# Last column group of the up projections in the merged form, first half of the down projections in a turning bank

## The reference, cut to what matters

```python
D_MODEL, SEQ, D_FF = 1024, 256, 2816
def conv_ffn(h, w_up, conv_w, conv_b, w_down):      # FFN 0 and 1
    gu = h @ w_up                                    # 1024 -> 2 * 2816
    g, u = gu[..., :D_FF], gu[..., D_FF:]
    g = depthwise_causal_conv(g, conv_w) + conv_b
    return (jax.nn.silu(g) * u) @ w_down             # 2816 -> 1024
def swiglu(x, w13, w2):                              # FFN 2 to 5
    gate, up = jnp.split(x @ w13, 2, axis=-1)
    return (jax.nn.silu(gate) * up) @ w2
```

## Time and profile before

| | us |
|---|---|
| median of 3 runs | 2125.82 |
| lowest and highest | 2122.11 and 2129.02 |
| the profiled execution | 2125.66 |
| its span in the profile | 2123.9 |

### The profile page before, as it was taken

How to read it: one execution, slowest core, us unless ns; L and a number is a source line. 1 busy time by engine, 2 the same in 40 slices (tenths; PEclk the granted TensorE clock), 3 DMA queues, 4 the chain that set the end, 5 groups by cost and what they waited for, 6 DMA issues and landing times.

```text
span 2123.9 us, 34246 instructions
## 1 busy us (share of the span) xinstructions
PE 2067.6 (97%) x14836; PEld 1801.3 (85%) x14836; DVE 1433.9 (68%) x1652; ACT 1055.2 (50%) x1256; POOL 155.4 (7%) x119
## 2 busy tenths in 40 slices
PE   8899999999999999999999999999999999999998
PEld 7888888988888888998778888888889977788887
DVE  7966766567765664876766776476558576678654
ACT  4545554655643553455544455345435564444542
POOL 1000000000001000330000010020005200002000
PEclk9799999999999999999999999999999999999999
DMA  7254655435555665563402466566546533135653
GB/s 186 40 169 153 198 189 172 156 119 179 179 188 189 197 199 178 186 206 126 139 23 100 156 205 195 188 189 198 180 161 217 197 119 119 43 119 167 210 189 129
DMA packets 259789, 342.45 MB, mean 161 GB/s; under 512 B 23383, under 2 KB 169469, under 8 KB 259639
## 3 DMA queue, kind: packets, MB, share of 16 engines
q1 hardware_dynamic: 254272, 329.95, 47.7%
q0 software_dynamic: 2768, 9.08, 1.5%
q10 hardware_dynamic: 2599, 1.23, 0.5%
HBM read 338.14 MB, written 2.10 MB: 160 GB/s over the span
## 4 chain that ended last, share of the span: by engine, by line
PE 77%; DVE 14%; ACT 4%; DMA 3%; issue 1%; POOL 0%; ACTq 0%; SPq 0%; DVEq 0%
PE acc L1969 10%; PE acc L1971 10%; PE acc L1970 10%; PE trp L2139 9%; PE acc L2139 7%; DVE w_lo L1244 5%; PE trp L2140 4%; PE acc L2140 4%; PE acc L1985 3%; PE trp L1969 2%; PE trp L1971 2%; PE trp L1970 2%; ACT w_hi L750 2%; PE acc L2034 1%; PE acc L2186 1%
## 5 line engine op out<-in xcount | busy, mean ns | idle before, releaser
L1244 DVE TENSOR_TENSOR w_lo<-raw,w_hi 128x2048 fp32r<-128x2048 f32 (+1 forms) x312 | 721.4, 2315 | 400.3 <-ACT w_hi L750 398.5
L750 ACT ACTIVATE w_hi<-raw 128x2048 fp32r<-128x2048 f32 (+1 forms) x312 | 586.2, 1880 | 526.3 <-PE acc L1971 182.0
L2139 PE MATMUL trp<-xT,w_hi 128*128 128x512 f32 x960 | 339.5, 398 | 0.8 <-DVE w_lo L1244 0.8
L2139 PE MATMUL acc<-xT,w_hi 128*128 128x512 f32 x768 | 271.3, 397 | 0.0
L2140 PE MATMUL trp<-xT,w_lo 128*128 128x256 f32 x960 | 268.9, 280 | 0.0
L2139 PEld LDWEIGHTS trp<-xT,w_hi 128*128 128x128 f32 x960 | 180.3, 188 | 45.6 <-issue 1.7
L2140 PE MATMUL acc<-xT,w_lo 128*128 128x256 f32 x768 | 215.1, 280 | 0.0
L1969 PE MATMUL acc<-w_hi,hT_hi 128*128 128x512 f32 x528 | 205.5, 389 | 0.0
L1970 PE MATMUL acc<-w_lo,hT_hi 128*128 128x512 f32 x528 | 205.5, 389 | 0.0
L1971 PE MATMUL acc<-w_hi,hT_lo 128*128 128x512 f32 x528 | 205.4, 389 | 0.0
L1969 PE MATMUL acc<-xT,w_hi 128*128 128x256 f32 x704 | 199.9, 284 | 3.5 <-DVE w_lo L1244 3.4
(11 more groups left out here) (436 smaller groups left out, 3430.8 us busy)
## 6 DMA issues: line engine op xcount, KB each, us to landing
raw<-in_ffn_w SPq DMA_DIRECT2D x184, 512.0 KB
raw<-in_w_in SPq DMA_DIRECT2D x60, 1024.0 KB
raw<-in_ffn_w_up SPq DMA_DIRECT2D x88, 512.0 KB
raw<-in_ffn_w SPq DMA_DIRECT2D x40, 1024.0 KB
raw<-in_ffn_w_down SPq DMA_DIRECT2D x20, 1024.0 KB
raw<-in_ssm_w_glu SPq DMA_DIRECT2D x16, 512.0 KB
raw<-in_kv_w SPq DMA_DIRECT2D x8, 1024.0 KB
raw<-in_w_branch_a SPq DMA_DIRECT2D x8, 1024.0 KB
```

The lines of the kernel that those rows point to most:

```text
L750: A(w_hi[:, p % SPL, 0:kt, :], raw[:, p % RAW, 0:kt, :], ACT.Copy).then_inc(hi_ready, 1)
L1244: V_.tensor_tensor(w_lo[:, p % SPL, 0:kt, :], raw[:, p % RAW, 0:kt, :], w_hi[:, p % SPL, 0:kt, :].bitcast(F32), ALU.subtract).then_inc(lo_ ...
L2139: mm(tile, w_hi[:, p % SPL, k, c], xT[:, k0 + k], start=i == k == 0, stop=False, skip_group_check=True)
```

## The change

Group 10 of all six up projections takes the merged form: it fills both `acc`, is folded like the groups before it, and uses one more number of `acc`. The first half of each down projection (j = 0 of `tokens`) no longer has a number of `acc`. It accumulates in `turn_banks[0]`, waits before its first matmul until group 9 is folded, and is released by `turn_freed`, for which TensorE also waits at the end of the FFN. The number of uses of `acc` per FFN stays the same, and so does the accumulator that the second half takes.

```diff
--- before.py
+++ after.py
@@ -50,7 +50,7 @@
 RAW, SPL = 2, 3
 TRP = 4
 
-MERGED = range(1, 10)
+MERGED = range(1, 11)
 
 TWO_PI = 2 * math.pi
 MAGIC = 1.5 * 2 ** 23
@@ -390,6 +390,15 @@
                     filled[n_use] = (panel_used, ps[-1] + 1)
                     n_use += 1
 
+        def down_uses(name):
+
+            nonlocal n_use
+            turns.append((name, 0))
+            pairs_at[name, 0] = None
+            pairs_at[name, 1] = n_use
+            filled[n_use] = (panel_used, gemms[name][1][-1] + 1)
+            n_use += 1
+
         def place(name, j):
 
             return pairs_at[name, j] if (name, j) in pairs_at else use[name] + j
@@ -404,7 +413,7 @@
         use["y"] = n_use
         n_use += 2
         gemm_uses("glu")
-        up_uses("up0"), gemm_uses("down0")
+        up_uses("up0"), down_uses("down0")
         spots = {}
 
         def turn_spot(name, k):
@@ -420,9 +429,9 @@
             turn_spot(f"rem{i}", 0), turn_spot(f"rem{i + 1}", 1), uses(f"rem{i + 2}", 1), uses(f"rem{i + 3}", 1)
         uses("oT", 2)
         gemm_uses("o")
-        up_uses("up1"), gemm_uses("down1")
+        up_uses("up1"), down_uses("down1")
         for i in range(DEPTH):
-            up_uses(f"up{2 + 2 * i}"), gemm_uses(f"down{2 + 2 * i}")
+            up_uses(f"up{2 + 2 * i}"), down_uses(f"down{2 + 2 * i}")
             uses(f"win{i}", SIDE, f"win{i}")
             uses(f"bdT{i}", 1), uses(f"bd{i}", 1), uses(f"G{i}", 1)
             for n in range(8 + 2):
@@ -441,7 +450,7 @@
                     uses(f"Z{i}_{lv}_{t}", 1)
             uses(f"dl{i}", 7)
             gemm_uses(f"brB{i}"), gemm_uses(f"wo{i}")
-            up_uses(f"up{3 + 2 * i}"), gemm_uses(f"down{3 + 2 * i}")
+            up_uses(f"up{3 + 2 * i}"), down_uses(f"down{3 + 2 * i}")
 
         def side_panel(i, n):
 
@@ -531,7 +540,11 @@
             return f * len(MERGED) + j - MERGED.start + 1
 
         def A2(u):
-            return acc[u % 2][:, :].rearrange("p (t n) -> p t n", t=2)
+            return (turn_banks[0] if u is None else acc[u % 2])[:, :].rearrange("p (t n) -> p t n", t=2)
+
+        def turn_no(name, j):
+
+            return turns.index((name, j)) + 1
 
         def A8(u):
             return acc[u % 2][:, :].rearrange("p (h m) -> p h m", h=8)
@@ -1335,6 +1348,14 @@
                     return V_.scalar_tensor_tensor(xs, xs, scale, A2(u)[:, ts], ALU.mult, ALU.add)
 
                 def evacuate(j, u):
+                    if u is None:
+                        dve.wait_ge(panel_used, gemms[name][j][-1] + 1)
+                        if nat is not None:
+                            dve.wait_ge(sem("xnat_ready"), naturals[nat] + 1)
+                        add(u, j, slice(0, TT)).then_inc(sem("turn_freed"), 1)
+                        dve.wait_ge(sem("turn_freed"), turn_no(name, j))
+                        statistics(j)
+                        return
                     if j < len(gemms[name]) - 1:
                         wait_filled(dve, u)
                         if nat is not None:
@@ -2019,7 +2040,10 @@
             def tokens(name, j, u, src, ready=None, arriving=None):
 
                 out = A2(u)
-                claim(u)
+                if u is None:
+                    pe.wait_ge(sem("turn_freed"), turn_no(name, j) - 1)
+                else:
+                    claim(u)
                 for i, p in enumerate(gemms[name][j]):
                     pe.wait_ge(lo_ready, p + 1)
                     _, _, k0, kt, _ = panels[p]
@@ -2148,8 +2172,9 @@
                     else:
                         features(f"up{f}", j, place(f"up{f}", j), xs, arriving=Arriving(xname))
                 for j in range(2):
-                    tokens(f"down{f}", j, use[f"down{f}"] + j, hT,
+                    tokens(f"down{f}", j, place(f"down{f}", j), hT,
                            lambda k0, kt: pe.wait_ge(sem("hlo_ready"), f * 11 + (k0 + kt) // 2))
+                pe.wait_ge(sem("turn_freed"), turn_no(f"down{f}", 0))
 
 
             pe.wait_ge(sem("ident_in"), 16)
```

## The result

The changed kernel takes 2128.67 us (median of 22 runs, 2125.23 to 2131.57), the kernel before 2125.9 beside it: ratio 1.0013, interval 1.0007 to 1.0019. It is 2.8 us slower, where 0.14 us less was forecast. Measured again beside other kernels it came to 1.0017 (1.0009 to 1.0026).

What follows compares the result with a forecast made beforehand. TensorE was taken to bound the kernel, with VectorE setting FFN 0's end. FFN 1 to 4 at -0.84, FFN 5 at -0.40 and FFN 0 at +1.1 gave -0.14 us against 2125.66: 2125.5 us, range 2121.5 to 2129.5.

Steps and rivals of the forecast that it cites:

- D2's stall: FFN 0's down projection, first half: TensorE waits 0.3 to 0.5 us for the late split of its third weight panel.
- the tail of FFN 0: End of FFN 0, which hangs on VectorE: its first addition comes 0.6 to 1.9 us later than 348.55.
- the tail of FFN 1: End of FFN 1: delayed loads regain 1.6 us before the end; loss 0, with 0.5 us as upper bound.
- Part 1: Groups 10 of six FFN: 96 matmuls become 64 each, gaining 1.49 us in all if TensorE sets the end.
- Part 3: Down projection's first half in the turning bank: costs 0, bound 0.05 us per FFN above and below.
- Part 2, FFN 0: Group 10's fold in FFN 0 delays a split by 1.93 us; loss 1.1 us, ends -0.1 and +3.1.
- the ring: Weight loads and splits releasing each other, 9.3 us a lap; in FFN 0 its delay was to reach the end.
- D4's load: Load of the down projection's fifth panel, 6.28 us in FFN 0: at 5.0 the delay is 0.65, at 6.28 1.93.
- Part 2, FFN 1: Group 10's fold in FFN 1, margin about 1 us at the third panel: cost 0, at most 0.5 us.
- nothing moves: Rival for the whole kernel: neither fold nor form shows, half-clock stretches come and go; 2124 to 2127.5 us, within 0.05.
- The weight loads: Rival: weight loads bind group 10, each group gives back 1.72 us, six times 10.3: 2115.3 us; chance 0.03.
- The clock rival: Rival: the new TensorE stall in FFN 0 halves the granted clock, costing 6.8 us: 2132.3 us; chance 0.05.

Runs made afterwards that it cites:

- the bank alone: Kernel before with all groups 10 plain and only the first half of every down projection accumulating in the turning bank: ratio 1.0003 (0.9995 to 1.0012).

## Why the prediction was wrong

Against the sum of the prediction, in means of the profiles: the groups 10 gave -1.69 (forecast -1.49), D2's stall and the tail of FFN 0 +1.62 (+1.35, which is the loss of 1.1 without the gain of 0.25), the tail of FFN 1 +0.87 (0), layer 0's mixer +4.82 (no term), and everything else -2.52 (no term), of which -1.89 is the rate of the merged pairs and -0.54 layer 1's mixer. Together +3.1 for -0.14. So two steps failed: FFN 1's tail was taken at nothing, and the stages behind the FFN were taken as unchanged. The measured 2128.67 us lies inside the stated range of 2121.5 to 2129.5 us, but only because that range was as wide as the spread of single runs; it bears out none of the mechanisms.

**Part 1** held: 0.21 in FFN 1 and 2, 0.21 or 0.42 in FFN 3 to 5 by the rate of the pairs, and 1.3 to 1.7 in all for 1.49.

**Part 3** held: the bank alone is 1.0003. Its use (without it the first half of each down projection lasts 1.8 to 6.4 us longer, the 6.4 with 6.8 us at half clock in it) was not in my text, since the trace of before can't show it.

**Part 2, FFN 0** held in mechanism; the size is partly luck: D2's split at 300.46 (300.42 forecast), the first half of the down projection 0.45 us longer (stall of 0.3 to 0.5 forecast), the delay carried by the ring. In the first profile little of the delay arrives: D4's load took 4.91 us, near the end of the range at which I had put the delay at 0.1, and the first addition is 0.31 us late. The tail brings another 0.0 to 2.6, by profile, and 1.7 of the 2.6 is a stretch at half clock. With the gain of group 10 the mean is -0.3 + 0.5 + 1.1 = +1.3, for +1.1; without that stretch it is +0.7.

**Part 2, FFN 1** failed: I took 0, at most 0.5, "a ring delayed by 1.6 us regains that before the end". D2's split starts 1.94 us later in relation to group 9's end, the last one 0.77 later in relation to group 10's, and the next stage 0.6 to 1.3 later. ScalarE's idle time of 4.38 us was not the slack of the ring. It ended with a slot of TensorE, but the load had landed only 0.96 us earlier, at 654.81: so 0.96 us was the slack, for a delay of 1.9 us. Idle time shows how long an engine has nothing to do, not how early its other input lay ready. I had named the signature, the tail of FFN 0 in FFN 1, as what would prove me wrong.

**What was not in the sum at all** is the largest term: the place of the instruction fetches, +4.8 us in layer 0 with the half clock that came with it. I priced an instruction removed by what it costs in the stream where it stands. The profile of before had the hint: in both delta rules TensorE waits 1.7 us for "issue" among the small matmuls, once each, four matmuls apart in their order. With 64 instructions fewer per group such waits had to move, and with them up to 4 us for each layer. A rival of that size on either side was missing; "nothing moves" held only the half-clock stretches, and took them as chance: up to 1.7 us each way.

**The weight loads and the clock.** The weight loads don't bind: group 10 kept 11.31 us. The clock rival didn't come as told: the stall at D2 left the clock at 1.00 in the stretch around it. Stretches of 3.4 us at half clock did come in other places, behind the hole in layer 0, once in the input projection and once behind FFN 0 (at 358.2 us).

I wrote that 0.3% is about what a measurement can tell. 22 runs of each told 0.13% with an interval of 0.06 on either side; for the sizes that this change deals in, that was the bound to think in.

## What to carry to other kernels

An edit that changed TensorE's number of instructions shifted the borders of its fetch blocks through all that followed, and cost time 200 us away from the edit. Where the stream is dense with tiny instructions, look in the profile for idle time that ends in "issue", and test the edit at two or three shifts before it is called slower or faster. A null edit, a whole block of increments, is the control.

Idle time in front of an instruction is slack only as long as its second input is early: look at what else it waits for, and when that arrived.

Where a loss has a new wait in it, look at the granted clock behind the wait too: here the half clock added nearly as much as the hole itself.

## What the runs showed of the hardware

The place of an instruction fetch among small matmuls. 64 instructions without work on TensorE cost 6.6 us (1.0031), 256 cost none that can be told (1.0001). The waits end 2.2 to 2.9 us after the transfer of a block began, though the transfer takes about 1 us; the wait of 2.0 to 2.3 us is where it began only 0.1 to 0.4 us before TensorE fell idle.

The merged pair has two rates. One profile goes from the one to the other at most a few times, mostly between FFN. Busy time by stretch, groups 1 to 9 of FFN 4, in the kernel before and in the changed one:

```profile
1408.02:1509.78 101.76, 101.76 (x578) 88.30 (x577) 71.05 (x53) 53.51 (x53) 13.02 (x6) 1.00 0.65 206
```

```profile
1413.40:1513.36 99.96, 99.96 (x577) 88.05 (x577) 70.94 (x53) 53.44 (x53) 13.07 (x6) 1.00 0.66 210
```

That is 353 and 347 ns for a pair, at a granted clock of 1.00 in both, and 1.8 us for an FFN. The changed kernel's third profile has the slow rate in all of FFN 3 to 5, its second the fast one. The gain of 0.40 that I read off for FFN 5 was 0.21 by the form and the rest by this rate: where the rate is slow, FFN 5 gains 0.21 too. What sets the rate stays open.
